# Splitting queries and keys in the projection stage of an encoder block, and a reordered program end

## Time and profile before

| | us |
|---|---|
| median of three executions | 2457.92 |
| lowest and highest | 2457.41, 2460.16 |
| the profiled execution | 2457.78 |
| its span in the trace | 2456.0 |
| mean granted clock of PE in it | 0.965 of full speed |

### The profile page before, as it was taken

One profiled execution on the slowest core, in us unless ns is written; L12 is line 12 of the kernel. 1 busy time (PEld: TensorE's weight loads), 2 busy tenths in 40 slices (PEclk: granted clock), 3 DMA queues, 4 the chain that ended last, 5 costly groups with the idle time before them and its releaser, 6 DMA issues.

```text
span 2456.0 us, 31260 instructions
## 1 busy us (share of the span) xinstructions
PE 2270.4 (92%) x11108; PEld 1861.4 (76%) x11108; DVE 1654.7 (67%) x2150; ACT 821.9 (33%) x1326; POOL 433.8 (18%) x273
## 2 busy tenths in 40 slices
PE   6999977888889998999899999999999999997995
PEld 4777866666677777787788888888888888875884
DVE  7667216877777774765777777777777777776545
ACT  5111006766665553312222212211212122135223
POOL 6101102222223333241000000000000000005101
PEclk9999997999999998999999999999999999998997
DMA  4211224121223320300110000100001000010102
GB/s 160 73 74 55 105 81 92 33 64 33 64 48 80 79 47 18 137 34 18 35 35 34 32 28 34 34 34 26 34 34 34 31 29 34 34 39 30 43 26 103
DMA packets 48989, 126.47 MB, mean 51 GB/s; under 512 B 20000, under 2 KB 20512, under 8 KB 48928
## 3 DMA queue, kind: packets, MB, share of 16 engines
q1 hardware_dynamic: 48064, 124.54, 16.6%
q10 hardware_dynamic: 864, 1.13, 0.1%
HBM read 105.20 MB, written 20.45 MB: 51 GB/s over the span
## 4 chain that ended last, share of the span: by engine, by line
PE 80%; DVE 10%; issue 5%; ACT 2%; DMA 1%; POOL 1%; DVEq 0%; ACTq 0%; SPq 0%; POOLq 0%
PE ps L286 22%; PE ps L287 21%; PE ps L288 21%; PE ps L876 4%; PE ps L852 3%; PE ps L882 3%; PE ps L841 2%; DVE PTL L1067 1%; PE ps L842 1%; DVE nmax L1046 1%; DVE NL L1649 1%; PE ps L860 1%; DVE QS L1013 1%; DVE osum L1087 1%; DVE WL L282 1%
## 5 line engine op out<-in xcount | busy, mean ns | idle before, releaser
L286 PE MATMUL ps<-NH,WH 128*128 128x512 f32 x1896 | 756.9, 399 | 42.9 <-DVE WL L282 30.9
L287 PE MATMUL ps<-NL,WH 128*128 128x512 f32 x1896 | 743.4, 392 | 0.0
L288 PE MATMUL ps<-NH,WL 128*128 128x512 f32 x1896 | 742.8, 392 | 0.0
L286 PEld LDWEIGHTS ps<-NH,WH 128*128 128x128 f32 x1896 | 359.4, 190 | 128.1 <-issue 36.1
L287 PEld LDWEIGHTS ps<-NL,WH 128*128 128x128 f32 x1896 | 359.6, 190 | 79.7 <-issue 6.0
L288 PEld LDWEIGHTS ps<-NH,WL 128*128 128x128 f32 x1896 | 359.1, 189 | 75.9
L263 POOL TENSOR_TENSOR raw<-raw,gains 128x1024 f32<-128x1024 f32 x78 | 154.9, 1992 | 1342.3 <-DMA raw<-in_w 1331.8
L1581 DVE TENSOR_TENSOR H<-H,ps 128x512 f32<-128x512 f32 x480 | 305.5, 682 | 103.2 <-PE ps L288 103.2
L278 ACT ACTIVATE WH<-raw 128x1024 fp32r<-128x1024 f32 x104 | 110.0, 1058 | 668.6 <-PE ps L288 665.7
L852 PE MATMUL ps<-ident,PR 128*128 128x128 f32 (+1 forms) x1056 | 169.3, 290 | 51.2 <-DVE PTL L1067 45.7
L286 PE MATMUL ps<-MH,WH 128*128 128x512 f32 x504 | 197.0, 391 | 6.7 <-DVE H L1656 6.7
(11 more groups left out here) (152 smaller groups left out, 3047.5 us busy)
## 6 DMA issues: line engine op xcount, KB each, us to landing
raw<-in_w SPq DMA_DIRECT2D x102, 512.0 KB, 3.2
qraw<-qkv SPq DMA_DIRECT2D x32, 384.0 KB, 5.2
kraw<-qkv SPq DMA_DIRECT2D x32, 384.0 KB, 7.5
qkv<-ob SPq DMA_DIRECT2D x9, 768.0 KB, 3.6
xst<-in_xT SPq DMA_DIRECT2D x24, 256.0 KB, 3.7
vraw<-qkv SPq DMA_DIRECT2D x16, 384.0 KB, 8.3
H<-in_xT SPq DMA_DIRECT2D x8, 768.0 KB, 8.8
out_yT<-H SPq DMA_DIRECT2D x24, 256.0 KB, 2.0
```

The lines of the kernel that those rows point to most:

```text
L286: nc.tensor.matmul(out, wh, xh, start=first, stop=False)
L287: nc.tensor.matmul(out, wh, xl, start=False, stop=False)
L288: return nc.tensor.matmul(out, wl, xh, start=False, stop=last)
```

## The change

Four things change.

1. In stage one every query and key tile is split where it is made. ACT rounds it (`high_plain`, `high_head`) into `oah`, `obh` or `oqh`, DVE makes the low part (`low_plain`, `low_head`), for plain tiles in the place of the value. The factor of the queries is applied there. Both parts are stored as rows of `qkh` and `qkl`; value tiles go to `qkv` as before. All bodies of SP, ACT and DVE are written out; PE keeps its loop.
2. In stage two SP loads the halves straight into `QS`, `KH`, `KL`; the work of `keys`, `queries`, `keys_low` and `queries_low` is gone. Group A's keys and values are loaded and the values turned once. The first head's queries and keys and both heads' values are loaded in stage one's seventh body, into buffers of their own. The first loads of group B have buffers of their own too. The waits for the stores of stage one move from its end into stage two's SP queue. Two weights of stage three are loaded and scaled in stage two.
3. In stage two ACT squares both heads' output of a token group at once (at m = 3, 19 and 23), POOL only adds. The loops are cut at item 4 and not at item 2.
4. In stage five the rows of groups 0 and 1 are copied one unit earlier, a square root on one element loads its table after the last sigmoid, the last reciprocal comes after three scalings of group 1, and DVE scales six tiles of group 1 where it scaled five.

```diff
+            store_plain(0, 1)
+            for i in range(1, BODIES):
+                if i < BODIES - 1:
+                    load_weight(sp, i * 2 + 2, 0)
+                    load_weight(sp, i * 2 + 3, 1)
+                if i >= NA_TILES:
+                    store_plain(i, 0)
+                if i <= NA_TILES:
+                    store_head(i - 1)
+                store_plain(i, 1)
+                if i == NA_TILES + 1:
+                    sp.wait_ge(st_h, 32 * NA_TILES)
...
+                    load_queries("A", 0, 0)
+                    load_keys("A", 0, 0)
+                    for s in range(2):
+                        load_values("A", 0, s)
...
             def body(i):
                 split_hi(act, i * 2 + 1, 1, i * 2 + 2)
...
+                if i >= NA_TILES:
+                    high_plain(i, 0)
+                if i <= NA_TILES:
+                    high_head(i - 1)
+                high_plain(i, 1)
...
+                if i >= NA_TILES:
+                    for g in range(G):
+                        low_plain(i, 0, g)
+                if head:
+                    rotary(i - 1, 1)
+                    low_head(i - 1, 0)
                 out_plain(i, 0, 1)
+                if head:
+                    rotary(i - 1, 2)
+                    low_head(i - 1, 1)
                 out_plain(i, 1, 1)
+                low_plain(i, 1, 0)
+                if head:
+                    low_head(i - 1, 2)
                 out_plain(i, 2, 1)
+                low_plain(i, 1, 1)
+                low_plain(i, 1, 2)
...
+            load_keys("A", 0, 1)
+            load_queries("A", 0, 1)
+            load_weight(sp, OUT0, 0)
+            load_weight(sp, OUT0 + 1, 1)
+            sp.wait_ge(st_a, stores_before(BODIES, 0))
+            sp.wait_ge(st_b, stores_before(BODIES, 1))
+            sp.sem_inc(all_stored, 1)
...
+            with sp.Fori(1, NPAIR_A) as i:
+                for s in range(2):
+                    scored(i - 1, s)
+                    load_queries("A", i, s)
...
+            with sp.Fori(1, NPAIR_B) as i:
+                for s in range(2):
+                    scored(i + (NPAIR_A - 1), s)
+                    load_queries("B", i, s)
+                    load_keys("B", i, s)
+                    sp.wait_ge(t_rdy[1], fills("B", i + (NPAIR_A - 1), ("V", s)))
+                    load_values("B", i, s)
+                    load_table(i, s)
...
-                    pe.wait_ge(q_lo[s], p * G + G)
-                    pe.wait_ge(k_lo[s], p + 1)
+                    pe.wait_ge(q_ld[kind][s], queries_landed(kind, p))
+                    pe.wait_ge(k_ld[kind][s], keys_landed(kind, p))
...
-            values(0, 0)
             scores("A", 0, 0)
+            values("A", 0, 0)
             scores("A", 0, 1)
+            values("A", 0, 1)
             every_pair(pe, step)
...
-                if m in (2, 3, 4):
-                    keys(p, 1, m - 2)
-                if m in (5, 6, 7):
-                    queries(p, 1, m - 5)
-                if m in (11, 12, 13) and after:
-                    keys(p + 1, 0, m - 11)
-                if m in (14, 15, 16) and after:
-                    queries(p + 1, 0, m - 14)
+                if m == 3 and before:
+                    square(p - 1, 2)
+                if m == 19:
+                    square(p, 0)
+                if m == 23:
+                    square(p, 1)
...
+            act.wait_ge(zeroed, 6)
+            exps("A", 0, 0)
             values("A", 0, 0)
-            exps("A", 0, 0)
             exps("A", 0, 1)
+            values("A", 0, 1)
...
+                if u_ == 6 * NQ - 1:
+                    nc.scalar.activation(warm[:], eps[:], ACT.Sqrt).then_inc(warmed, 1)
...
+                    if q == NQ - 1 and x == 5:
+                        rms_row(act, ROW6 + 2, ROW_BANKS[1], rstd_h[:, cols(1)])
                     unit(q, x)
...
-            for g in range(1, G):
-                if g == 2:
-                    group_recip(dve, CALL6, 2)
-                dve.wait_ge(st_ok, ROW6 + g + 1)
-                scaled(g, range(Y_DVE[g]))
+            dve.wait_ge(st_ok, ROW6 + 2)
+            scaled(1, range(3))
+            group_recip(dve, CALL6, 2)
+            scaled(1, range(3, Y_DVE[1]))
+            dve.wait_ge(st_ok, ROW6 + 3)
+            scaled(2, range(Y_DVE[2]))
```

More of the change, by code:

```diff
@@ L625, in body @@
+            def body(i):
+                head = i <= NA_TILES
+                first = out_plain if i >= NA_TILES else (lambda i, g, _: out_a(i, g))
                 split_lo(dve, i * 2 + 1, 1)
-                head_norm(i - 1, 0)
+                if head:
+                    head_norm(i - 1, 0)
                 first(i, 0, 0)
-                head_norm(i - 1, 1)
+                if head:
+                    head_norm(i - 1, 1)
                 first(i, 1, 0)
-                rotary(i - 1, 0)
@@ L769, in s2_sync, with load_table @@
-            for s in range(2):
-                load("A", 0, 0, s, first=True)
+            def load_table(i, s):
+                sp.wait_ge(tab[1 - s], i * 4 + 2 * s + TAB_FREE)
+                for half in range(2):
+                    src = bass.AP(tensor=a["rpb_tensor"], offset=(i * 2 + s) * (RPB_R * RPB_C) + RPB_C * (1 - half),
+                                  ap=[[1, GRID], [RPB_C, 14], [1, GRID]])
+                    nc.sync.dma_start(TR[cols(half, GRID), :, :], src).then_inc(t_ld[s], 16)
@@ L978, in step @@
                 else:
-                    act.wait_ge(t_rdy[1], fills(p, ("T", m)))
+                    act.wait_ge(t_rdy[1], fills(kind, p, ("T", m)))
                 if m + 2 < ITEMS:
@@ L2008, in program @@
     a["qkv"] = nc.dram_tensor("qkv", (N_IN, P, T), F32, kind="Internal").ap()
+    for name in ("qkh", "qkl"):
+        a[name] = nc.dram_tensor(name, (N_IN, P, T), F32, kind="Internal").ap()
     a["yT"] = nc.dram_tensor("out_yT", (D, T), F32, kind="ExternalOutput").ap()
```

402 lines of the change are left out of this document (203 added, 199 removed).

## The result

The changed kernel takes **2397.47 us** (median of 4 runs, 2396.31 to 2400.41) beside 2458.28 us for the kernel before on the same chip: a ratio of **0.9753**, 95% interval 0.9737 to 0.977. The profiled execution is the one of 2396.31 us; its span is 2394.2 us, 61.8 less than before.

A forecast was written before the change was run, and what follows sets the result against it. PE bounds stage one and group B; no engine fills group A, bound by a ring, and PE idles at the hand-over. Savings 17.2 + 34 + 3 + 3 = 57 from 2457.8 give 2400.6 us; range 2381 to 2426, likeliest case about 2390 to 2412.

The forecast's parts named there:

- Hand-over: Between stages one and two: last vector result to item 2's nmax takes 11.0 us instead of 28.2, 17.2 saved.
- The chain of three parts: At the hand-over: barrier 0.5, six memsets 3.7 and the way to item 2's nmax 6.8, in sum 11.0 us.
- Stage one: Added splits raise ACT to some 48 us and DVE to some 134; cost 0, with 0 to 5 for a stall.
- Group A: First attention group: disturbed stretches priced as undisturbed ones of the same shapes, less 3.7 for squares: 34 us saved.
- 8 to 12 as long as 20 to 24: Sign in group A's pairs: these two stretches of four items, of the same shapes, become equally long.
- ring: Group A's time is a cycle: scores on PE, nmax on DVE, exponential on ACT, transposes on PE, split on ACT and DVE.
- the rival of 2420: Group A's ring closes on something else; stretches save only removed query splits less squares, 18 us: 2420 us, chance 0.23.
- The clock rival: Shorter gaps in group A keep PE at full clock, 10 to 12 us more saved: 2388 us, chance 0.12.
- Group B: Second attention group: the same splits go, but PE idles only 6.4 us in three pairs; 3 us saved (0 to 8).
- To stage three: Way into stage three: last square moves from POOL to ACT, two weights are scaled earlier; costed at nothing.
- End: Program end: last reciprocal after three scalings comes 4.6 us earlier, a table load may cost 0 to 1.6; 3 saved.
- The squares' table swap: Case of table loads at ACT's squares in attention, between exponentials; the one case not faster; chance 0.04.

The follow-up runs named there:

- h2_loads: Changed kernel, but stage one waits for its last stores at its end and group A's first queries, keys and values load only in stage two: 2409.85 us.
- b2_weight: Changed kernel with stage three's third weight loaded ahead of the eight hidden-state loads, not behind them: 2393.11 us.
- u1_squares: Changed kernel with the squares of attention's output back on POOL and none on ACT: 2401.18 us.
- x2_act: Changed kernel with twelve 128x512 ACT copies put back in each pair of group A, into a buffer nobody reads: 2396.93 us.
- best: Changed kernel with third weight ahead of hidden state, memset wait moved to item 3, last unit's row copy behind the last sigmoid: 2391.64 us.
- e1_end: Changed kernel with the program end's old order: later row copies, last reciprocal behind five scalings, no early square-root table load: 2400.86 us.

## Why the prediction was right

2400.6 was forecast and 2397.47 measured, inside the range and inside the likeliest case. That the two are only 3 us apart is in part luck: 3.4 and 4.1 us more than forecast in the two groups and 1.6 at the end stand against 4.2 lost in stages three to five, on which nothing was put, and 0.9 at the hand-over; inside group A errors of 4 to 6 us cancel too. By its steps:

*Hand-over, 17.2 for 16.3.* The chain of three parts was right; the 6.8 us for the way to item 2 came out 7.05 (358.69 to 365.74), and barrier and memsets 4.8 (353.89 to 358.69) for 4.2. h2_loads gives the loads' and stores' share alone, 12.4 us (13.3 in its trace).

*Stage one, 0 for 0.* DVE 130 and ACT 43 for the forecast 134 and 48. Weights 16 and 17 were scaled from 311.80, near the 315 forecast, and PE did not stall.

*Group A, 34 for 37.4.* Replacing each disturbed stretch by its twin worked: a pair without an episode measures 73.8 (pair 0 of b2_weight), for 74.8. Two terms were mis-sized and one wasn't there. The squares were charged 3.7 and cost 0 (u1_squares); the stretches of 12.3, taken for undisturbed, held query copies on ACT and are 11.8 (x2_act brings 12.40 back); and the episodes that are left, one in each pair at 1.4 to 1.5 us, take back some 6. For this reason the sign "8 to 12 as long as 20 to 24" did not come: 13.55 and 15.22. The reasons behind the old pair's stretches are shown, with one seam. The value fills are 3.6 and 1.6 us, an episode among the 3.6 that no trace separates; the short vector operations are 0.8 and 0.9, POOL's subtraction beside one of them 2.1, ACT's copies 0.6 and 0.3; and the 12.86 of items 12 to 16 is 11.3 and an episode (0.87). The prediction took this last one, and others, for work that the change removes. The bet was between ring and instruction time: the rival of 2420 fell because it priced only the query splits and left out the value fills, which were worth 14.3 us of A.

*The clock rival* was true in its mechanism, as a part of the 37.4 and not as 12 us on top of the 34: the clock is 0.97 for 0.93, four episodes for thirteen. Four of the thirteen, in items 16 to 20, cost nothing; of the rest five are gone, at 1.4 us some 7 us. The forecast had them in its twins without naming them.

*Group B, 3 for 7.1.* In pairs 4 to 6 the items from 16 to 20 fell from 11.15 to 9.17 and those from 20 to 24 rose from 9.02 to 9.86, 1.1 us in each: 3.4, which is the forecast. 1.3 more is an episode in pair 4's first four items (13.55 us before, 12.22 after). 2.0 lie in items 4 to 8, which are now 10.05, now 11.24 us long in kernels of the same code, by where POOL's addition falls; this trace had three short ones. Kernels with the same group B and no episode in it reach up to 240.6, which would be 4.9 saved.

*Stages three to five, 0 for -4.2: the term that was put at nothing.* 1.36 is the last unit: row copy and table load ahead of the last sigmoid, in every kernel with this end (8.29 from the root's table load to the last accumulation, for 6.93). The prediction had this (0 to 1.6) but booked it at the end. 2.3 is the third weight, of which the part "To stage three" doesn't speak: PE waited 2.5 us for it, 0.2 before. But in the eleven kernels (the changed one among them) that have this code alike, PE waited 0.3 to 2.7 us, so it belongs to how the transfers happen to fall and only b2_weight and best are rid of it. The last 0.5 is within what these stages differ by (1466.9 to 1473.3 over them).

*End, 3 for 4.6, less the 1.36.* 3.2 net, with which e1_end agrees (3.4), and not the 1.5 that the prediction feared for POOL's multiplications. Two scalings did take 2.41 us with POOL beside them and not 1.40, at 2373.78, but they end at 2376.19 and the last sigmoid at 2376.15: DVE had nothing else to do yet. In the last kernel, where the sigmoid is earlier, they are on the path.

*The squares' table swap* is false: one load at the first exponential, none at a square.

## What to carry to other kernels

Cut a loop that no engine fills into stretches of equal shapes and price a change by the difference between a disturbed stretch and its twin, not by the removed instructions' time: here 30 us of work on ACT were worth 3 in their own stretches, 17 us on DVE 7, and seven value fills 14 with an episode among them. Read each stretch's granted clock beside its length: stretches of the same work at the same clock agree to 0.1 us, and an episode more or less (1.4 us) can hide or mimic what is being measured. What a wait costs is PE's idle time behind it (2.5 us of 12.5), and an instruction moved off a path may let POOL loose beside the next one on it.
